# A weight slot given back in parts behind a pair of interleaved tiles

## The chip, the cores and the metric

The kernel runs on one core of one Trainium2 chip. The metric is the device time of one execution in microseconds (us), smaller is better. Five engines run side by side, each through its own list of instructions: TensorE (PE, matrix products), VectorE (DVE), ScalarE (ACT), GpSimd (POOL) and SyncE (SP, which here only starts transfers). They meet at counting semaphores alone. Matrix products land in PSUM, which has 8 banks of 512 floats per partition; two neighbouring banks are a "pair" here, and there are four pairs, 0 to 3.

## What is computed

Two transformer blocks over 1024 tokens of width 1024, in float32. Cut to what matters:

```python
# first block
xn   = rmsnorm(x) ; proj = xn @ w_in            # queries, keys, values, gated-delta inputs
h    = x + concat(windowed_attention, gated_delta_rule) @ w_out
h    = h + square(relu(rmsnorm(h) @ w_ffn_in)) @ w_ffn_out
# second block, on rmsnorm(h)
proj = rmsnorm(h) @ w_in_2                      # forgetting attention q k v f z, differential q k v z, gates
y    = gate_a * (ya @ w_branch[0]) + gate_b * (yb @ w_branch[1])
out  = h + rmsnorm(y @ w_out_2)
```

## The kernel before, in words

Every dense layer is cut into tiles of 128 output columns, numbered n = 0 to 159 through the whole program (N_OUT1 = 23, N_FFN = 31, N_FOX = 95 are the first tiles of the mixer's output, of the feed-forward layer and of the second block). A tile's weights are eight 128x128 blocks, one for each k of the 1024 input columns. Three steps bring a tile to PE:

- SP loads them into the raw slot `Wraw[:, n % 2]` (512 KB), once the tile two before has been split.
- POOL splits them into a rounded part and a remainder: a cast `Wh <- Wraw`, then a subtraction `Wl <- Wraw, Wh`. It may start when PE has finished tile n - 2, which used the same slot (semaphore `mm_done`), and posts `w_ready` when done.
- PE makes the tile with 48 matmuls: for each k three products (`Wh` by the high and by the low part of the input, `Wl` by the high part), each over two halves of 512 tokens. This is `product`. It waits for `w_ready` and, through `ps_free`, for the PSUM pair n % 2 to have been emptied by DVE or ACT.

Ordinarily PE makes one tile while POOL splits the next. At the start of four layers the input comes k by k from DVE and ACT. There `product_two` makes two tiles at once: for each k six matmuls of tile n, then six of tile n + 1. So both slots stay taken until the last k. These four places are called here by the tile pair made together: A (tiles 0 and 1, phase 1), B (N_OUT1, phase 5), C (N_FFN, phase 7) and D (N_FOX, phase 9).

In phase 1 the first five tiles are keys and queries. Their weights are loaded by `load_q` in two pieces whose rows are 64 floats long, on semaphores `q_in`, and split by `split_q`. Their results go to scratch memory (`bk_scr`, `bq_scr`) and come back as `bk` (`load_keys`, two transfers of 1 MB) and `bq` (`load_queries`). SP starts all of these in a written order and stops at each wait in it, so what stands behind a wait starts later. After tile 5 PE begins the windowed attention (`scores`, first matmul on line 676), with tiles 6 to 22 filled in between its steps.

In phase 9 two short matmul groups with `ones` spread per-token factors over the partitions: one (line 350) into pair 3, which DVE reads while it makes the input; and one (line 1875, from `dg1`) into pair 2, which DVE reads later, when it scales `hT`. DVE waits for the second one (`ms_done` 6) ahead of its first `st_l`, the operation that empties a PSUM pair there (line 1941) after ACT's `st_h` (line 1892).

Of the kernel before, what the change touches and what calls it, by code (L numbers as in the profile page):

```python
# [19 lines left out]
ALU = mybir.AluOpType  # L20
# [82 lines left out]
def build(nc, a, out):  # L103
    ctx = ExitStack()
    with ctx:
# [11 lines left out]
        def sem(name):  # L117
            return ctx.enter_context(nc.semaphore(name))
# [57 lines left out]
        def pair(s):  # L176
            return PS[:, 2 * s:2 * s + 2, :].rearrange("p b n -> p (b n)")
# [93 lines left out]

        def product(pe, n, slot, xs, x_ready=None):

            pe.wait_ge(w_ready, n + 1)
            if not (isinstance(n, int) and n < 2):
                pe.wait_ge(ps_free, n - 1)
            for c, (k, hi, lo) in enumerate(xs):
                if x_ready:
                    x_ready(k)
                for w, x, m in ((Wh, hi, 0), (Wh, lo, 1), (Wl, hi, 2)):  # L280
                    for b in range(2):
                        mm = pe.matmul(PS[:, 2 * slot + b, :], w[:, slot, k], x[:, b * 512:(b + 1) * 512],  # L282
                                       start=(c == 0 and m == 0), stop=(c == len(xs) - 1 and m == 2))
            mm.then_inc(mm_done, 1)
# [87 lines left out]
        def split_dve(dve, s0, w, row, spread=None):  # L372
# [23 lines left out]
            low(KT - 1)  # L396

        def product_two(pe, n, xs, ready, halves=False):

# [3 lines left out]
            for c, (k, hi, lo) in enumerate(xs):  # L403
# [10 lines left out]
                for i in range(2):  # L414
                    slot = (n + i) % 2
                    for w, x, m in ((Wh, hi, 0), (Wh, lo, 1), (Wl, hi, 2)):
                        for b in range(2):
                            mm = pe.matmul(PS[:, 2 * slot + b, :], w[:, slot, k], x[:, b * 512:(b + 1) * 512],  # L418
                                           start=(c == 0 and m == 0), stop=(c == len(xs) - 1 and m == 2))
                    if c == len(xs) - 1:  # L420
                        mm.then_inc(mm_done, 1)

        const_in, vec_in, x_in = sem("const_in"), sem("vec_in"), [sem(f"x_in{i}") for i in range(4)]
        par_in, filled = sem("par_in"), mixer_sem("filled")
        xT_done, xT_act, xT_dve = sem("xT_done"), sem("xT_act"), sem("xT_dve")
        pv_psum = sem("pv_psum")
        spill, x_back = sem("spill"), sem("x_back")
# [41 lines left out]
        def pe_phase0(pe):  # L469
# [12 lines left out]
            pe.wait_ge(vec_in, N_VEC)  # L482
            pe.transpose(PS[:, 4, 0:V_ROWS], vecs[:], ident[0:V_ROWS, 0:V_ROWS]).then_inc(pv_psum, 1)
            pe.wait_ge(acc_done, 1)
# [18 lines left out]
        def dve_phase0(dve):  # L503
# [3 lines left out]
            for g in BY_DVE:  # L507
                half, k = g // KT, g % KT
                dve.wait_ge(xT_done, g + 1)
                dve.tensor_copy(hT[:, k, half * 512:half * 512 + 512], PS[:, g % 4]).then_inc(xT_dve, 1)  # L510
            dve.wait_ge(pv_psum, 1)
            dve.tensor_copy(pv[:], PS[:, 4, 0:V_ROWS])
# [54 lines left out]
        def sp_phase1(sp):  # L567
# [6 lines left out]
            sp.wait_ge(line_sb, 1)  # L574
            sp.dma_start(line_one, line[:]).then_inc(line_out, 16)
            sp.wait_ge(bs_out[0], 32)
            load_keys(sp)
            sp.wait_ge(w_ready, 3)
            load_q(sp, 4)
            load_group(sp, N_ATT + 5, 1, a["w_in"], 640, loop=False)  # L580
# [49 lines left out]
        def pool_phase1(pool):  # L630
            pool.memset(cpad[0][:, 0:2], 0.0)
            pool.memset(cpad[0][:, S + 2:S + 4], 0.0)
            for j in range(2, 5):
                split_q(pool, j)
# [1018 lines left out]
        def pool_phase7(pool):  # L1653
            split(pool, N_FFN + 2, N_FOX + 2)

# [198 lines left out]
        def pool_phase9(pool):  # L1854
            split(pool, N_FOX + 2, N_VA)
            split_values(pool, N_VA, (va_h, va_l))

        h_final, m2_done = late_sem("h_final"), late_sem("second_norm_sum")
        dg1 = sb("dg1", [P, S], F32, R + 72)

        def pe_phase9(pe):
# [7 lines left out]
            for b in range(2):  # L1869
                pe.wait_ge(acc_done, 4 + b)  # L1870
                spread_half(pe, pair(3), facc[0], b).then_inc(ms_done, 1)
            product_two(pe, N_FOX, model, lambda k: pe.wait_ge(x_ready, 18 + k + 2), True)
            pe.wait_ge(acc_done, 6)
            for b in range(2):
                mm = pe.matmul(PS[:, 4 + b], ones[:], dg1[:, b * 512:(b + 1) * 512], start=True, stop=True)
            mm.then_inc(ms_done, 1)
            pairs(pe, N_FOX + 2, 6, lambda n, j, slot: product(pe, n, slot, model))
            product(pe, N_FGT, N_FGT % 2, model)
            value_products(pe, N_VA, (va_h, va_l))

        def act_phase9(act):
# [38 lines left out]
        def dve_phase9(dve):  # L1920
# [815 lines left out]
```

## Time and profile before

| what | value |
|---|---|
| median of 3 runs | 2551.58 us (2550.88 to 2552.43) |
| the profiled execution | 2553.9 us, of which the span of the trace is 2552.1 us |
| PE busy | 2441.5 us, 96% of the span |
| POOL busy | 689.7 us, 27% |
| DVE, ACT busy | 1002.2 us (39%), 723.1 us (28%) |
| mean granted TensorE clock | 0.972 of full |

A busy share of 96% leaves about 110 us in which PE does nothing. Each such stretch shows in the timeline of PE as an idle time in square brackets, with the instruction that ended it. Times in the timeline are microseconds from the span's start; the second number of a row is how long its group of instructions lasted. Steady pairs of 512-column matmuls start every 0.453 us, so one takes 0.227 us at full clock, and a tile of 48 takes 10.88 us.

### The profile page before, as it was taken

How to read it: one execution, taken by the hardware profiler on the slowest of the kernel's cores; microseconds unless marked ns; L12 is line 12 of the kernel's file. 1: busy time of each engine (PE TensorE's matmuls, PEld its weight loads, DVE VectorE, ACT ScalarE, POOL GpSimd, SP SyncE). 2: the span in 40 equal slices, each digit the busy share in tenths (PEclk: the TensorE clock that was granted, in tenths of full speed). 3: DMA queues.
4: the chain of work that ended last, by engine and by line, in shares of the span. 5: the costliest groups of instructions: out<-in, count | busy, mean ns of one | idle time of the engine just before them, and what ended most of it. 6: DMA issues, size and time to landing. Idle time of an engine off the chain costs nothing.

```text
span 2552.1 us, 33188 instructions
## 1 busy us (share of the span) xinstructions
PE 2441.5 (96%) x13182; PEld 2077.6 (81%) x13182; DVE 1002.2 (39%) x1479; ACT 723.1 (28%) x1147; POOL 689.7 (27%) x423
## 2 busy tenths in 40 slices
PE   6999996899898999999999999999999999999997
PEld 5788886899876888888888877988888788887886
DVE  4176634455535312212213344123333343557533
ACT  4144554122412100101101121135443113655022
POOL 2221112343322433333334322321111231111321
PEclk8999997899898999999999989999999999999998
DMA  6722212322330111111111115523441346524422
GB/s 206 205 58 67 67 51 68 92 57 57 133 107 25 58 50 42 49 49 49 49 49 49 47 35 187 169 62 91 120 118 51 130 165 145 134 65 149 149 91 91
DMA packets 257967, 232.11 MB, mean 91 GB/s; under 512 B 43233, under 2 KB 228359, under 8 KB 256312
## 3 DMA queue, kind: packets, MB, share of 16 engines
q1 hardware_dynamic: 234680, 170.65, 23.7%
q10 hardware_dynamic: 23168, 59.81, 6.5%
q8 instruction: 82, 1.34, 0.2%
q14 instruction: 37, 0.30, 0.0%
HBM read 167.41 MB, written 65.11 MB: 91 GB/s over the span
## 4 chain that ended last, share of the span: by engine, by line
PE 92%; DVE 2%; ACT 1%; DMA 1%; issue 1%; POOL 1%; POOLq 0%; ACTq 0%; DVEq 0%; SPq 0%; PEldq 0%; PEld 0%
PE PS L282 40%; PE PS L301 18%; PE PS L1828 4%; PE PS L2478 3%; PE PS L418 3%; PE PS L1783 3%; PE PS L2034 2%; PE PS L1320 2%; PE PS L1326 2%; PE PS L698 1%; PE PS L2023 1%; PE PS L2317 1%; PE PS L676 1%; PE PS L1337 1%; PE PS L686 1%
## 5 line engine op out<-in xcount | busy, mean ns | idle before, releaser
L253 POOL CAST Wh<-Wraw 128x1024 fp32r<-128x1024 f32 x144 | 150.8, 1047 | 1469.0 <-PE PS L282 619.3
L255 POOL TENSOR_TENSOR Wl<-Wraw,Wh 128x1024 fp32r<-128x1024 f32 x144 | 375.6, 2608 | 20.7
L1702 ACT ACTIVATE rbuf<-PS 128x1024 f32<-128x1024 f32 x32 | 32.9, 1028 | 493.7 <-PE PS L282 483.2
L282 PE MATMUL PS<-Fl,Wh 128*128 128x512 f32 x512 | 157.6, 389 | 0.0
L282 PE MATMUL PS<-Fh,Wh 128*128 128x512 f32 x512 | 157.6, 389 | 0.0
L282 PE MATMUL PS<-Fh,Wl 128*128 128x512 f32 x512 | 157.6, 389 | 0.0
L282 PE MATMUL PS<-XAh,Wh 128*128 128x512 f32 x440 | 139.7, 399 | 13.0 <-POOL Wl L255 6.0
L301 PE MATMUL PS<-XAh,Wh 128*128 128x512 f32 x328 | 134.8, 411 | 2.1 <-POOL Wl L255 2.1
L282 PE MATMUL PS<-XAl,Wh 128*128 128x512 f32 x440 | 136.1, 391 | 0.0
L282 PE MATMUL PS<-XAh,Wl 128*128 128x512 f32 x440 | 135.9, 390 | 0.0
L282 PE MATMUL PS<-XBh,Wh 128*128 128x512 f32 x440 | 135.5, 389 | 0.0
L282 PE MATMUL PS<-XBl,Wh 128*128 128x512 f32 x440 | 135.4, 389 | 0.0
L282 PE MATMUL PS<-XBh,Wl 128*128 128x512 f32 x440 | 135.4, 389 | 0.0
L301 PE MATMUL PS<-XAl,Wh 128*128 128x512 f32 x328 | 135.0, 412 | 0.0
L301 PE MATMUL PS<-XAh,Wl 128*128 128x512 f32 x328 | 134.6, 410 | 0.0
L301 PE MATMUL PS<-XBl,Wh 128*128 128x512 f32 x328 | 134.2, 409 | 0.0
L301 PE MATMUL PS<-XBh,Wh 128*128 128x512 f32 x328 | 133.6, 407 | 0.0
L301 PE MATMUL PS<-XBh,Wl 128*128 128x512 f32 x328 | 133.4, 407 | 0.0
L1732 DVE TENSOR_TENSOR rbuf<-rbuf 128x1024 f32<-128x1024 f32 x32 | 41.4, 1293 | 210.1 <-ACT rbuf L1702 210.1
L1742 DVE TENSOR_TENSOR hT<-hT,PS 128x1024 f32<-128x1024 f32 x24 | 29.3, 1221 | 218.3 <-PE PS L282 218.3
L282 PEld LDWEIGHTS PS<-Fl,Wh 128*128 128x128 f32 x512 | 96.1, 188 | 19.9
L282 PEld LDWEIGHTS PS<-Fh,Wl 128*128 128x128 f32 x512 | 96.1, 188 | 19.9
(431 smaller groups left out, 5416.4 us busy)
## 6 DMA issues: line engine op xcount, KB each, us to landing
Wraw<-in_w_in SPq DMA_DIRECT2D x66, 512.0 KB, 4.4
Wraw<-in_w_ffn_in SPq DMA_DIRECT2D x32, 512.0 KB, 4.0
Wraw<-in_w_ffn_out SPq DMA_DIRECT2D x32, 512.0 KB, 4.0
x_scr<-hT SPq DMA_DIRECT2D x2, 4096.0 KB, 14.2
Wraw<-in_w_out SPq DMA_DIRECT2D x16, 512.0 KB, 4.1
gate_scr<-gbuf ACTq DMA_DIRECT2D x16, 512.0 KB, 2.6
gin<-gate_scr ACTq DMA_DIRECT2D x8, 1024.0 KB, 7.3
xtok<-in_x SPq DMA_DIRECT2D x4, 1024.0 KB, 8.3
```

What stands on the lines that cost most here:

```text
L253: pool.tensor_copy(Wh[:, slot], Wraw[:, slot])
L255: pool.tensor_tensor(Wl[:, slot], Wraw[:, slot], Wh[:, slot].bitcast(F32), ALU.subtract).then_inc(w_ready, 1)
L282: mm = pe.matmul(PS[:, 2 * slot + b, :], w[:, slot, k], x[:, b * 512:(b + 1) * 512], start=(c == 0 and m == 0), stop=(c == len(xs) - 1 and ...
L301: mm = pe.matmul(PS[:, b, :], w[:, slot, k], x[:, b * 512:(b + 1) * 512], start=(c == 0 and m == 0), stop=(c == KT - 1 and m == 2))
L418: mm = pe.matmul(PS[:, 2 * slot + b, :], w[:, slot, k], x[:, b * 512:(b + 1) * 512], start=(c == 0 and m == 0), stop=(c == len(xs) - 1 and ...
L1320: mm = pe.matmul(bank(d, e)[:, h * 64:(h + 1) * 64], KdTs[p % 2][e][d][:, h], joined(W_of(p, e, d)[:, h], n, d), start=True, stop=True)
L1326: mm = pe.matmul(bank(d, e)[:, h * 64:(h + 1) * 64], U_of(p, e, d)[:, h], Xs[e][d][:, h, 0:64], start=True, stop=True)
L1732: dve.tensor_tensor(rbuf[:], rbuf[:], rbuf[:], ALU.mult).then_inc(f_sq, 1)
L1783: mm = pe.matmul(dst(c)[:, 0:w * P], q[:, i * P:(i + 1) * P], x[:, c * 512:c * 512 + w * P], start=(x is kh), stop=(x is kl and c != i // 4))
L1828: mm = pe.matmul(dst, x[:, at], w[:, :, k], start=(c == 0 and m == 0), stop=(c == KT - 1 and m == 2))
L2034: mm = pe.matmul(PS[:, 7, i * HD:(i + 1) * HD], aPT[:, p % 2, b * P:(b + 1) * P], vtok[:, k, h * HD:(h + 1) * HD], start=(k == 0), stop=(k ...
L2478: mm = pe.matmul(PS[:, 4 * (j % 2) + 2 * (k // 4) + b, :], w[:, slot, k], x[:, b * 512:(b + 1) * 512], start=(k % 4 == 0 and m == 0), stop ...
```

## The change

`product_two` posts a new semaphore, `first_parts`, when tile n has used its first six k blocks (`EARLY = 6`). POOL splits the next tile for that slot (n + 2) in two parts, by the new `split_behind_two`: blocks 0 to 5 on `first_parts`, blocks 6 and 7 on `mm_done` as before. This is done at all four places. In phase 1 SP now starts the load of tile 4 ahead of the keys. In phase 9 the spreading matmuls of `dg1` go ahead of `product_two`, and tile N_FOX + 2 is written to pair 3 instead of its usual pair, with ACT and DVE reading it there (`fox_bank`). One semaphore is saved by counting a transpose on `xT_done`.

```diff
-        def product(pe, n, slot, xs, x_ready=None):
+        def product(pe, n, slot, xs, x_ready=None, taken=None):
             pe.wait_ge(w_ready, n + 1)
-            if not (isinstance(n, int) and n < 2):
+            bank = slot
+            if taken is not None:
+                slot = n % 2
+                pe.wait_ge(ps_free, taken)
+            elif not (isinstance(n, int) and n < 2):
                 pe.wait_ge(ps_free, n - 1)
...
-                        mm = pe.matmul(PS[:, 2 * slot + b, :], w[:, slot, k], x[:, b * 512:(b + 1) * 512],
+                        mm = pe.matmul(PS[:, 2 * bank + b, :], w[:, slot, k], x[:, b * 512:(b + 1) * 512],
...
+        EARLY = 6
...
                     if c == len(xs) - 1:
                         mm.then_inc(mm_done, 1)
+                    elif c == EARLY - 1 and i == 0:
+                        mm.then_inc(first_parts, 1)
+
+        def split_behind_two(pool, n, x):
+            s = n % 2
+            for part, free, count in ((slice(0, EARLY), first_parts, x + 1), (slice(EARLY, KT), mm_done, n - 1)):
+                pool.wait_ge(free, count)
+                pool.tensor_copy(Wh[:, s, part], Wraw[:, s, part])
+                pool.drain()
+                ins = pool.tensor_tensor(Wl[:, s, part], Wraw[:, s, part], Wh[:, s, part].bitcast(F32), ALU.subtract)
+            ins.then_inc(w_ready, 1)
...
             sp.dma_start(line_one, line[:]).then_inc(line_out, 16)
+            sp.wait_ge(w_ready, 3)
+            load_q(sp, 4)
             sp.wait_ge(bs_out[0], 32)
             load_keys(sp)
-            sp.wait_ge(w_ready, 3)
-            load_q(sp, 4)
...
-            for j in range(2, 5):
+            pool.wait_ge(q_in[0], 64)
+            split_behind_two(pool, 2, 0)
+            for j in range(3, 5):
                 split_q(pool, j)
...
-            split(pool, N_OUT1 + 2, N_FFN + 2)
+            pool.wait_ge(w_in[N_OUT1 % 2], landed(N_OUT1 + 2))
+            split_behind_two(pool, N_OUT1 + 2, 1)
+            split(pool, N_OUT1 + 3, N_FFN + 2)
...
+        def fox_bank(j):
+            return pair(3 if j == 2 else (N_FOX + j) % 2)
...
-            product_two(pe, N_FOX, model, lambda k: pe.wait_ge(x_ready, 18 + k + 2), True)
             pe.wait_ge(acc_done, 6)
             for b in range(2):
                 mm = pe.matmul(PS[:, 4 + b], ones[:], dg1[:, b * 512:(b + 1) * 512], start=True, stop=True)
             mm.then_inc(ms_done, 1)
-            pairs(pe, N_FOX + 2, 6, lambda n, j, slot: product(pe, n, slot, model))
+            product_two(pe, N_FOX, model, lambda k: pe.wait_ge(x_ready, 18 + k + 2), True)
+            product(pe, N_FOX + 2, 3, model, taken=N_FOX)
+            product(pe, N_FOX + 3, (N_FOX + 3) % 2, model)
+            pairs(pe, N_FOX + 4, 4, lambda n, j, slot: product(pe, n, slot, model))
```

Places C and D have the same edit of POOL's list as B. What it makes of that list, for POOL at place A (tiles 2, 3 and 4), before and then now:

```order
L621 CAST Wh<-Wraw 128x1024 [waits mm_done,q_in0]
L623 TENSOR_TENSOR Wl<-Wraw,Wh 128x1024
L621 CAST Wh<-Wraw 128x1024 [waits mm_done,q_in1]
L623 TENSOR_TENSOR Wl<-Wraw,Wh 128x1024
L621 CAST Wh<-Wraw 128x1024 [waits mm_done,q_in0]
```

```order
L436 CAST Wh<-Wraw 128x768 [waits first_parts,q_in0]
L438 TENSOR_TENSOR Wl<-Wraw,Wh 128x768
L436 CAST Wh<-Wraw 128x256 [waits mm_done]
L438 TENSOR_TENSOR Wl<-Wraw,Wh 128x256
L639 CAST Wh<-Wraw 128x1024 [waits mm_done,q_in1]
L641 TENSOR_TENSOR Wl<-Wraw,Wh 128x1024
L639 CAST Wh<-Wraw 128x1024 [waits mm_done,q_in0]
```

Only tile 2 is split in two parts; tiles 3 and 4 wait as they did. SP's list in phase 1, where lines 443 and 461 are the loads of `load_q` and lines 606 and 624 those of the keys, before and then now:

```order
L575 DMA line_one<-line 8x512
L606 DMA bk<-bk_scr 64x4x1024 x2
L443 DMA Wraw<-in_w_in 128x8x64 x2
L208 DMA Wraw<-in_w_in 128x8x128
L582 DMA line_scr<-line_one 128x4096
```

```order
L593 DMA line_one<-line 8x512
L461 DMA Wraw<-in_w_in 128x8x64 x2
L624 DMA bk<-bk_scr 64x4x1024 x2
L208 DMA Wraw<-in_w_in 128x8x128
L600 DMA line_scr<-line_one 128x4096
```

Tile 4's two pieces have passed the two key transfers and nothing else. PE's list in phase 9, with the spread of `dg1` on line 1875 before and 1903 now; in between stand the remaining matmuls of `product_two` (line 418, now 424). First before:

```order
L350 MATMUL PS<-facc_138,ones 128x512 x2
L410 MATMUL PS<-XAh,Wh 128x512
...
L418 MATMUL PS<-XBh,Wl 128x512 x2
L1875 MATMUL PS<-dg_157,ones 128x512 x2
L195 UNCONDITIONAL_BRANCH
L195 ISA
L276 REGISTER_ALU
L282 MATMUL PS<-XAh,Wh 128x512 x2
```

Now:

```order
L354 MATMUL PS<-facc_138,ones 128x512 x2
L1903 MATMUL PS<-dg_157,ones 128x512 x2
L416 MATMUL PS<-XAh,Wh 128x512
...
L424 MATMUL PS<-XBh,Wl 128x512 x2
L286 MATMUL PS<-XAh,Wh 128x512 x2
```

The spread has moved from behind the pair of tiles to ahead of it, and the loop that held six tiles starts two tiles later.

## Rows read from the trace of the kernel before

**Rows 1.** Timelines of POOL, DVE, PE at A: start, us, engine, line, operation, [idle before].

```profile
53.95 1.04 POOL L621 CAST Wh<-Wraw 128x1024 fp32r<-128x1024 f32 x1 [26.51 <-PE PS L418]
54.96 1.23 DVE L825 SCALAR_TENSOR_TENSOR bst_l<-PS,bst_h 128x1024 fp32r<-128x1024 f32 x1 [7.48 <-ACT bst_h L738]
55.09 1.02 PE L652 MATMUL PS<-onehot,relb 33*8 33x512 f32 x2
57.53 0.73 PE L282 MATMUL PS<-XAh,Wh 128*128 128x512 f32 x2 [1.41 <-POOL Wl L623]
```

**Rows 2.** One line's instructions on POOL: duration in ns, least, median, most.

```profile
L645 POOL TENSOR_TENSOR Wl<-Wraw,Wh x1: 461/461/461, 351.0 to 351.0; 128x128 fp32r<-128x128 f32 x1
```

**Rows 3.** Timeline of PE: tile 3's end, tile 4, tile 5, the first scores.

```profile
78.97 0.61 PE L282 MATMUL PS<-XBh,Wl 128*128 128x512 f32 x2
83.78 1.22 PE L282 MATMUL PS<-XAh,Wh 128*128 128x512 f32 x2 [4.19 <-POOL Wl L623]
...
96.31 0.61 PE L282 MATMUL PS<-XAh,Wh 128*128 128x512 f32 x2
...
109.31 0.72 PE L676 MATMUL PS<-bk,bq 128*128 128x256 f32 x4
```

**Rows 4.** Timeline of SP's queue in phase 1: start and time to issue.

```profile
61.33 1.70 SPq L606 DMA_DIRECT2D bk<-bk_scr  x2
63.08 4.60 SPq L443 DMA_DIRECT2D Wraw<-in_w_in  x2
...
88.00 0.37 SPq L588 DMA_DIRECT2D bias<-line_scr  x1
104.18 2.58 SPq L614 DMA_DIRECT2D bq<-bq_scr  x4
```

**Rows 5.** DMA issues, windows 63:67.6, 40:43, 82.3:83, 99.2:100: KB, median us to landing.

```profile
Wraw<-in_w_in SPq DMA_DIRECT2D x2, 256.0 KB, 14.8
...
Wraw<-in_w_in SPq DMA_DIRECT2D x2, 256.0 KB, 6.1
...
bq_scr<-bst_l ACTq DMA_DIRECT2D x1, 512.0 KB, 8.1
...
bq_scr<-bst_l ACTq DMA_DIRECT2D x1, 512.0 KB, 4.9
```

**Rows 6.** Timelines of PE and DVE at B.

```profile
720.16 0.61 PE L418 MATMUL PS<-XBh,Wl 128*128 128x512 f32 x2
721.59 2.35 DVE L1639 TENSOR_TENSOR hT<-hT,PS 128x1024 f32<-128x1024 f32 x2 [12.20 <-DMA hT<-x_scr]
723.26 0.72 PE L282 MATMUL PS<-XAh,Wh 128*128 128x512 f32 x2 [2.49 <-POOL Wl L255]
```

**Rows 7.** Timelines of POOL, ACT and PE at C.

```profile
824.76 1.04 POOL L253 CAST Wh<-Wraw 128x1024 fp32r<-128x1024 f32 x1 [32.21 <-PE PS L418]
825.95 3.36 POOL L255 TENSOR_TENSOR Wl<-Wraw,Wh 128x1024 fp32r<-128x1024 f32 x1
...
824.81 1.03 ACT L1702 ACTIVATE rbuf<-PS 128x1024 f32<-128x1024 f32 x1 [8.28 <-PE PS L418]
...
829.44 0.73 PE L282 MATMUL PS<-XAh,Wh 128*128 128x512 f32 x2 [3.49 <-POOL Wl L255]
```

**Rows 8.** Timelines of PE and DVE at D.

```profile
1517.84 3.78 PE L350 MATMUL PS<-facc,ones 128*128 128x512 f32 x4 [2.65 <-DVE facc L361]
1524.35 0.76 PE L410 MATMUL PS<-XAh,Wh 128*128 128x512 f32 x1 [2.73 <-DVE XAl L378]
...
1547.69 1.88 PE L1875 MATMUL PS<-dg,ones 128*128 128x512 f32 x4
1550.94 0.73 PE L282 MATMUL PS<-XAh,Wh 128*128 128x512 f32 x2 [1.38 <-DVEq L1944]
...
1518.30 1.22 DVE L1935 TENSOR_TENSOR dg<-ident,sp 128x1024 f32<-128x1024 f32 x1
```

**Rows 9.** Windows at D: busy us of each engine, granted clock (PEclk), DMA share, GB/s.

```profile
1518.00:1524.00 6.00, 3.62 (x4) 1.01 (x4) 4.61 (x6) 1.63 (x3) 0.00 (x0) 0.50 0.00 0
1527.00:1528.00 1.00, 1.00 (x5) 0.78 (x4) 0.91 (x2) 0.26 (x1) 0.00 (x0) 0.79 0.00 0
```

More of the change, by code:

```diff
@@ L425, in build @@
         xT_done, xT_act, xT_dve = sem("xT_done"), sem("xT_act"), sem("xT_dve")
-        pv_psum = sem("pv_psum")
+        first_parts = sem("first_parts")
         spill, x_back = sem("spill"), sem("x_back")
@@ L482, in pe_phase0 @@
             pe.wait_ge(vec_in, N_VEC)
-            pe.transpose(PS[:, 4, 0:V_ROWS], vecs[:], ident[0:V_ROWS, 0:V_ROWS]).then_inc(pv_psum, 1)
+            pe.transpose(PS[:, 4, 0:V_ROWS], vecs[:], ident[0:V_ROWS, 0:V_ROWS]).then_inc(xT_done, 1)
             pe.wait_ge(acc_done, 1)
@@ L510, in dve_phase0 @@
                 dve.tensor_copy(hT[:, k, half * 512:half * 512 + 512], PS[:, g % 4]).then_inc(xT_dve, 1)
-            dve.wait_ge(pv_psum, 1)
+            dve.wait_ge(xT_done, 2 * KT + 1)
             dve.tensor_copy(pv[:], PS[:, 4, 0:V_ROWS])
@@ L1653, in pool_phase7 @@
         def pool_phase7(pool):
-            split(pool, N_FFN + 2, N_FOX + 2)
+            pool.wait_ge(w_in[N_FFN % 2], landed(N_FFN + 2))
+            split_behind_two(pool, N_FFN + 2, 2)
+            split(pool, N_FFN + 3, N_FOX + 2)
         def pe_phase7(pe):
@@ L1854, in pool_phase9 @@
         def pool_phase9(pool):
-            split(pool, N_FOX + 2, N_VA)
+            pool.wait_ge(w_in[N_FOX % 2], landed(N_FOX + 2))
+            split_behind_two(pool, N_FOX + 2, 3)
+            split(pool, N_FOX + 3, N_VA)
             split_values(pool, N_VA, (va_h, va_l))
+        def fox_bank(j):
+            return pair(3 if j == 2 else (N_FOX + j) % 2)
         h_final, m2_done = late_sem("h_final"), late_sem("second_norm_sum")
@@ L1891, in act_phase9 @@
                     act.wait_ge(qk_out[j % 2], 32 * (j // 2))
-                act.activation(st_h[:, j % 2], pair(n % 2), ACT.Copy, scale=-0.125 if j < 4 else 1.0).then_inc(qk_hi, 1)
+                act.activation(st_h[:, j % 2], fox_bank(j), ACT.Copy, scale=-0.125 if j < 4 else 1.0).then_inc(qk_hi, 1)
                 act.wait_ge(qk_hi, j + 1)
@@ L1940, in dve_phase9 @@
                 dve.wait_ge(qk_hi, j + 1)
-                dve.scalar_tensor_tensor(st_l[:, j % 2], pair((N_FOX + j) % 2), -0.125 if j < 4 else 1.0,
+                dve.scalar_tensor_tensor(st_l[:, j % 2], fox_bank(j), -0.125 if j < 4 else 1.0,
                                          st_h[:, j % 2].bitcast(F32), ALU.mult, ALU.subtract).then_inc(qk_lo, 1)
```

## The prediction

> **What bounds the kernel now.** I read the busy shares first: PE is busy for 96% of the span, so only the holes in PE's timeline, and stretches in which its clock is low, can be won back. Then I read PE's timeline around the four pairs of tiles. Each has a hole behind it, shown by the idle time in brackets: 1.41 us at A, 2.49 at B, 3.49 at C, 1.38 at D [rows 1, 6, 7, 8]. A fifth and largest hole, 4.19 us, stands ahead of tile 4 in phase 1 [rows 3]. Of each I then asked which wait ends next if the one named is removed, in the timelines of POOL, DVE and ACT, and for the fifth in SP's queue and the landings.
>
> **The slot given back in parts: POOL's side.** At A the split starts at 53.95, on the end of tile 0, about 1.1 us before PE's stream for the pair ends (the next matmul starts at 55.09). PE starts tile 2 at 57.53, so whole split and wake-up take 3.58 us [rows 1]: cast 1.04, a pause of 0.15 (824.76 + 1.04 to 825.95, [rows 7]), subtraction and wake-up 2.39. Now only two blocks of eight are left at that moment. Their cast is a quarter, 0.26; the pause stays; the subtraction lies between a quarter, 0.6, and what the 128-column one says: 0.46 for one block [rows 2] and about 0.27 for each further, so 0.73. With 0.1 for the wake-up that is 1.1 to 1.25; for a fixed cost in the cast I take 1.3. So the slot is ready 0.2 us after the pair ends. The first part, three quarters of 3.58 or 2.7 us, begins when 30 of the pair's 96 matmuls are left, 6.8 us at 0.227, and must be done in the 5.7 us before tile n's end: it is hidden, with 3 us to spare. It adds one cast, one subtraction and one pause to POOL, which idled for 26 us there [rows 1]. PE's matmuls are the same ones.
>
> **A, tile 2.** The slot is ready at 53.95 + 1.3 = 55.25. But tile 2 needs PSUM pair 0, which DVE has read at 54.96 + 1.23 = 56.19, and line 652 ends at 55.09 + 1.02 = 56.11 [rows 1]. So PE starts at 56.3: gain 57.53 - 56.3 = 1.2.
>
> **A, tile 4.** Its two pieces are issued at 63.08, behind 2 MB of keys, and take 14.8 us to land [rows 4, 5]; PE waits until 83.78, while tile 3's stream ends at 78.97 + 0.45 = 79.42 [rows 3]. Moved up, they are issued at 61.33, where the keys stood. PE now wants tile 4 at 79.42 - 1.2 = 78.2, so they must land by 78.2 - 3.6 = 74.6, 13.3 us after issue. The nearest row, pieces of this size behind another transfer that had just ended, took 6.1 [rows 5]; the same 14.8 as before would leave a hole of about 3 us. I take that the hole is gone: 4.36. It also cost clock: tile 4 took 96.31 - 83.78 = 12.53 instead of 10.88 [rows 3], because PE restarted at half clock; 1.65 comes back. A is now ahead by 1.2 + 4.36 + 1.65 = 7.2 at tile 5.
>
> What is late next there? The first scores (109.31, wanted at 102.1 now) need the keys, the bias and the first queries. The keys are started some 4 us later than 61.33 but wanted 36 us later: hidden. The queries are issued at 104.18, when the stores of tile 4's result have landed; the second store took 4.9 us from its issue at about 99.3 on an idle DMA, while the one before it, among other traffic, took 8.1 [rows 4, 5]. The stores now start 7.2 us sooner, at 92.1, beside the bias load that is issued at 88.00 and is not sooner. Between 4.9 and 8.1 I take 6.2, since the bias is then half landed: queries issued at 98.3 instead of 97.0. That is 1.3 late, of which some 0.4 was slack (their issue and landing end at about 108.9). PE waits 0.9. A gives 7.2 - 0.9 = 6.3; ends 4.0 (8.1 us store) and 7.2.
>
> **B.** Ready at 720.16 + 0.45 + 0.2 = 720.8 instead of 723.26. But tile N_OUT1 + 2 also needs PSUM pair 1 of tile N_OUT1, and DVE empties it only from 721.59, having waited 12.20 us for the 4 MB of `hT` to come back; its two operations take 2.35, the first ends at 722.8 [rows 6]. That DMA starts on DVE's work, which the change does not touch. PE starts at 722.9: gain 0.3, not 2.4.
>
> **C.** The split starts at 824.76; ready at 826.06 instead of 829.44. ACT empties the PSUM pair at 824.81 + 1.03 = 825.84 [rows 7], earlier. Gain 3.4. The subtraction took 3.36 us here and not 2.4: DVE squared `rbuf` at the same time. Now POOL's short subtraction starts at about 825.2, before ACT's copy has ended and so before DVE's square; if DVE came first, it would cost POOL one DVE operation, 1.2 us, and C would give 2.2. The SBUF — State Buffer page of the Trainium skill ("Who interferes with whom") says that DVE with two SBUF inputs and GpSimd lock one port pair against each other for a whole instruction, whoever starts first. By that rule C is 3.4 or 2.2, nothing between, and the longer subtraction in the trace agrees with it. The slot-1 split that now follows at once may hold DVE's square up; DVE has a whole tile, 10.9 us, for a chain of about 6.
>
> **D.** Before, three things stood between the pair's end (1547.69) and tile N_FOX + 2 (1550.94): the spread of `dg1`, 1.88 us; POOL; and DVE's emptying of the pair, which ended last [rows 8]. All three go: the spread moves ahead, the tile gets pair 3, POOL is ready 1.3 after a release at 1547.69 - 1.1 = 1546.6, so at 1547.9. That is 3.0 us. The price is the spread ahead of the pair. DVE has `dg1` ready at 1518.30 + 1.22 = 1519.5. PE's first spread ends at 1517.84 + 3.78 = 1521.62, and PE idles 2.73 us until 1524.35 [rows 8]. At half clock the moved one takes 3.78, as its twin does, and ends at 1525.4, 1.05 late; at full clock it takes 1.88 and fits. The granted clock is 0.50 (1.2 GHz) up to 1524 and rises to full (2.4 GHz) within 1527:1528 [rows 9], some 3 us after PE restarts at 1524.35. Behind the hole of tile 4 it rose after 1.65 / 0.5 = 3.3 us of half speed. Now PE runs without a hole from 1517.84, so by these two I expect full clock by about 1523, the moved spread done by 1524.35, and the first block of the pair (12 matmuls, before 7 slow and 5 fast, 4.1 us) at full clock, 2.7 us. Of that 1.4 I take 1.0, since DVE needs two operations of 1.2 us for the next block. Below, no earlier rise: 1.05 late, of which the 2.4 matmuls moved from half to full clock return half, so 0.55 lost; at worst 1.05. D gives 3.0 + 1.0 = 4.0; ends 2.0 and 4.4. TensorE: Matmul & The Clock Gate ("What's actually happening") in the Trainium skill says that activity releases the throttle. By that rule filling the hole makes the clock rise sooner and D is worth 4.0, without it 2.5; the half clock in [rows 9] while PE had holes agrees.
>
> **Sum.** 6.3 + 0.3 + 3.4 + 4.0 = 14.0 us. The loops that start a tile later, the dropped `slot_open` posts and the shared semaphore change instructions on engines that idle there: nothing. The profiled execution took 2553.9 us (2552.1 of span, 1.8 around it), which gives 2539.9. It was 2.3 above the median of 2551.58, so the median should be **2537.6 us**. Between the four places PE shows no hole in which an earlier start could be lost again before the next fixed event; a gain at one place is carried to the end.
>
> **Rivals.**
> 1. The clock at D does not rise sooner. For it: at D full clock came only at 1527, ten us after 1517.84. Against: a hole lay between. D gives 2.5, sum 12.5: 2539.1.
> 2. Phase 1 gives part back: the tile-4 pieces land late, or the stores beside the bias take 8.1 us and the first scores wait for queries. For it: the DMA rows of that stretch, 14.8 and 8.1 [rows 5]. A gives about 3.5, sum 11.2: 2540.4.
> 3. The change doesn't do what it says: the first part is not done when tile n ends, so the slot is ready as late as before. For it nothing in the rows; POOL has 5.7 us for 2.7. Then A gives 4.36 + 1.65 - 0.9 = 5.1, B and C nothing, D 1.7 (0.7, POOL's full split ending 3.6 after the release, and the 1.0 of the clock), sum 6.8: 2544.8.
> 4. Slower: the keys, now behind 2048 short rows and with the line table and bias behind them, land so late that `scores` waits. The order of bytes is the same for all but the keys, so it would take a queue that slows down as a whole. It decides from a landing past 102.1 and turns the sum negative only past 102.1 + 14 = 116, 35 us later than the slowest piece of before landed. At 120 it would be 2555.5.
>
> **How the numbers follow.** Forecast 0.62, rival 1 0.18, rival 2 0.14, rival 3 0.04, rival 4 0.02. The likeliest case alone spans 2536 to 2539. For the range: all best ends give 7.2 + 0.3 + 3.4 + 4.4 = 15.3, 2536.3, less a run's spread of 0.8, so 2535.3; the worst ends of A, C and D give 4.0 + 0.3 + 2.2 + 2.0 = 8.5, 2543.1. This leaves out rivals 3 and 4. About 0.2%, 5.1 us, is what a measurement of this kernel can tell from no change: faster by more than that 0.95, within it 0.03, slower 0.02.
>
> **What would show it.** In the trace after: tile 2 starting about 1.2 us behind the pair's end at A, held by DVE; no idle ahead of tile 4 and full clock through it; `bq` issued near 98; at B a hole of about 2.2 us that still ends with DVE and `hT`; at C and D holes under 0.5 us; full clock before 1525 less the shift at D. Wrong would be: a wait on `Wraw` ahead of tile 4, a wait of scores on keys or bias, a second part longer than 1.5 us, or a hole behind tile N_FOX + 2 or + 3 for PSUM.

## The result and the profile after

| | before | after |
|---|---|---|
| median of 5 runs each on one chip, us | 2552.43 (2550.88 to 2554.57) | 2539.39 (2537.82 to 2540.67) |
| ratio after / before, 95% interval | | 0.9948 (0.9937 to 0.9958) |
| profiled execution / its span, us | 2553.9 / 2552.1 | 2537.8 / 2536.0 |
| mean granted clock in the profile | 0.972 | 0.976 |

The kernel became 13.0 us faster by the medians and 16.1 by the two profiled executions; 14.0 was forecast, as 2537.6 us. The median came out 1.8 us above that, of which 0.85 is that the kernel before has a median of 2552.43 here and had one of 2551.58 there. Line numbers of the new kernel are 4 to 28 higher: L436 and L438 are the new split in parts, L286 and L424 the old L282 and L418, L672 the old L652.

**A.** Timelines of POOL, DVE and PE (start, us, engine, line, operation, [idle before <- who ended it]), the answer to [rows 1]:

```profile
47.28 0.83 POOL L436 CAST Wh<-Wraw 128x768 fp32r<-128x768 f32 x1 [20.03 <-PE PS L424]
48.25 1.85 POOL L438 TENSOR_TENSOR Wl<-Wraw,Wh 128x768 fp32r<-128x768 f32 x1
52.65 0.40 POOL L436 CAST Wh<-Wraw 128x256 fp32r<-128x256 f32 x1 [2.55 <-PE PS L424]
53.19 0.74 POOL L438 TENSOR_TENSOR Wl<-Wraw,Wh 128x256 fp32r<-128x256 f32 x1
```

```profile
53.73 1.23 DVE L845 SCALAR_TENSOR_TENSOR bst_l<-PS,bst_h 128x1024 fp32r<-128x1024 f32 x1 [6.45 <-ACT bst_h L758]
```

```profile
53.87 1.02 PE L672 MATMUL PS<-onehot,relb 33*8 33x512 f32 x2
55.16 0.70 PE L286 MATMUL PS<-XAh,Wh 128*128 128x512 f32 x2 [0.27 <-DVEq L848]
77.04 0.61 PE L286 MATMUL PS<-XAh,Wh 128*128 128x512 f32 x2
87.92 0.61 PE L286 MATMUL PS<-XAh,Wh 128*128 128x512 f32 x2
```

The first part is done at 50.10, the second at 53.93, six hundredths after L672 starts. PE is then held by DVE, until 54.96. Tile 4 starts at 77.04 with no idle time in its row and lasts 10.88 us, all of it at full clock; before it lasted 12.53 [rows 3].

SP's queue and the landings, the answer to [rows 4, 5], and what PE waits for then:

```profile
60.10 1.77 SPq L461 DMA_DIRECT2D Wraw<-in_w_in  x2
61.92 1.63 SPq L624 DMA_DIRECT2D bk<-bk_scr  x2
86.55 0.38 SPq L606 DMA_DIRECT2D bias<-line_scr  x1
97.35 2.59 SPq L632 DMA_DIRECT2D bq<-bq_scr  x4
```

```profile
Wraw<-in_w_in SPq DMA_DIRECT2D x2, 256.0 KB, 4.4
...
bq_scr<-bst_l ACTq DMA_DIRECT2D x1, 512.0 KB, 6.5
```

```profile
103.03 0.71 PE L696 MATMUL PS<-bk,bq 128*128 128x256 f32 x4 [1.86 <-DMA bq<-bq_scr]
...
104.97 0.38 PE L706 MATMUL PS<-ident,wS 128*128 128x128 f32 x2
```

```profile
101.88 1.28 ACT L799 ACT_TABLE_LOAD   x1
```

The pieces of tile 4 land 4.4 us after their issue (before 14.8) and the scores now wait 1.86 us for the queries. ACT's load of a table (the last fence) falls into that wait. L706 is the first turn of the scores: there PE transposes the first weights `wS`, which ACT has made behind that table.

**B.** Timelines of DVE and PE, the answer to [rows 6]:

```profile
712.99 0.61 PE L424 MATMUL PS<-XBh,Wl 128*128 128x512 f32 x2
...
715.81 0.95 PE L286 MATMUL PS<-XAh,Wh 128*128 128x512 f32 x2 [2.20 <-DVE hT L1661]
716.56 1.05 PE L286 MATMUL PS<-XAl,Wh 128*128 128x512 f32 x2
```

```profile
714.53 2.35 DVE L1661 TENSOR_TENSOR hT<-hT,PS 128x1024 f32<-128x1024 f32 x2 [12.33 <-DMA hT<-x_scr]
```

The hole is left, and DVE, which waits for `hT`, ends it. Two matmuls now take 1.05 us and not 0.62: PE restarts at half clock, which it did not in the profile before. The pair itself also took longer. Its start in PE's timeline, before and then now:

```profile
695.87 1.20 PE L418 MATMUL PS<-XAh,Wh 128*128 128x512 f32 x2
```

```profile
687.43 1.20 PE L424 MATMUL PS<-XAh,Wh 128*128 128x512 f32 x2
```

With its last matmul at 720.16 and at 712.99 that makes 24.74 us before and 26.01 now, with the rise to full clock later in it.

**C.** Timelines of POOL, PE and DVE, the answer to [rows 7]:

```profile
817.28 0.40 POOL L436 CAST Wh<-Wraw 128x256 fp32r<-128x256 f32 x1 [2.55 <-PE PS L424]
817.83 0.74 POOL L438 TENSOR_TENSOR Wl<-Wraw,Wh 128x256 fp32r<-128x256 f32 x1
```

```profile
818.70 0.72 PE L286 MATMUL PS<-XAh,Wh 128*128 128x512 f32 x2
```

```profile
820.85 3.39 DVE L1758 TENSOR_TENSOR Fl<-rbuf,Fh 128x1024 fp32r<-128x1024 f32 x1 [1.13 <-ACT Fh L1728]
```

POOL's short subtraction takes 0.74 us, as at A, and PE starts with no idle time in the row. The collision has moved: DVE's `Fl`, an operation that takes about 1.2 us alone, now takes 3.39 beside POOL's next split.

**D.** Timeline of PE, the answer to [rows 8], and the windows of [rows 9] (busy us of PE, PEld, DVE, ACT, POOL, then the granted clock):

```profile
1505.90 3.78 PE L354 MATMUL PS<-facc,ones 128*128 128x512 f32 x4 [2.65 <-DVE facc L365]
1509.48 2.87 PE L1903 MATMUL PS<-dg,ones 128*128 128x512 f32 x4
1512.41 0.47 PE L416 MATMUL PS<-XAh,Wh 128*128 128x512 f32 x1
...
1534.15 0.61 PE L424 MATMUL PS<-XBh,Wl 128*128 128x512 f32 x2
1534.81 0.73 PE L286 MATMUL PS<-XAh,Wh 128*128 128x512 f32 x2
```

```profile
1505.90:1508.50 2.60, 2.60 (x3) 1.18 (x4) 2.17 (x3) 0.00 (x0) 0.00 (x0) 0.50 0.00 0
1511.00:1513.00 2.00, 1.94 (x6) 0.86 (x5) 1.91 (x4) 1.19 (x2) 0.00 (x0) 0.89 0.00 0
```

The moved spread takes 2.87 us, between 3.78 (half clock, 1.2 GHz) and 1.88 (full, 2.4 GHz): the clock rises within it. The pair starts 6.51 us after the first spread, as it did before, but at full clock.

The same stretches in both profiles, in us, from the starts in PE's timeline:

| stretch | before | after | gain |
|---|---|---|---|
| A: pair's end (L672 starts) to tile 2 | 2.44 | 1.29 | 1.15 |
| tile 2 to tile 5 | 38.78 | 32.76 | 6.02 |
| tile 5 to the first turn of scores | 15.90 | 17.05 | -1.15 |
| B: the hole | 2.65 | 2.37 | 0.28 |
| B: the next six tiles | 65.43 | 66.99 | -1.56 |
| C: the hole | 3.66 | 0.29 | 3.37 |
| D: the pair | 23.33 | 22.19 | 1.14 |
| D: pair's end to next tile | 3.26 | 0.21 | 3.05 |
| pairs at A, B, C; column sums ahead of D | 87.52 | 85.09 | 2.43 |

In the last row the pairs at A and C and the column sums (short matmuls with `ones`) vary from profile to profile, as the runs below show; the pair at B (1.27 us longer now) is another matter, taken up under B further down.

### The profile page after: what moved, and what is told of

Its sections match the earlier page's. It is cut to its first block, busy times and chain, and to the rows that moved or that the text cites. A ratio compares the mean times of both kernels' runs of the same rounds, so it can differ in the third digit from the quotient of the medians.

```text
span 2536.0 us, 33223 instructions
## 1 busy us (share of the span) xinstructions
PE 2437.3 (96%) x13182; PEld 2073.2 (82%) x13182; DVE 997.9 (39%) x1479; ACT 723.1 (29%) x1147; POOL 691.3 (27%) x431
## 4 chain that ended last, share of the span: by engine, by line
PE 91%; DVE 3%; DMA 2%; ACT 1%; issue 1%; POOL 0%; POOLq 0%; DVEq 0%; SPq 0%; ACTq 0%; PEldq 0%; PEld 0%
PE PS L286 40%; PE PS L305 18%; PE PS L1852 4%; PE PS L2509 3%; PE PS L1807 3%; PE PS L2065 2%; PE PS L424 2%; PE PS L1346 2%; PE PS L1340 2%; PE PS L718 1%; PE PS L2054 1%; PE PS L2348 1%; PE PS L696 1%; PE PS L1357 1%; PE PS L706 1%
## 5 line engine op out<-in xcount | busy, mean ns | idle before, releaser
L255 POOL TENSOR_TENSOR Wl<-Wraw,Wh 128x1024 fp32r<-128x1024 f32 x141 | 367.5, 2607 | 20.3
L286 PE MATMUL PS<-Fh,Wl 128*128 128x512 f32 x512 | 157.6, 389 | 0.0
L286 PE MATMUL PS<-Fl,Wh 128*128 128x512 f32 x512 | 157.6, 389 | 0.0
L286 PE MATMUL PS<-Fh,Wh 128*128 128x512 f32 x512 | 157.6, 389 | 0.0
L286 PE MATMUL PS<-XAh,Wh 128*128 128x512 f32 x440 | 139.7, 399 | 2.6 <-DVE hT L1661 2.2
L286 PE MATMUL PS<-XAl,Wh 128*128 128x512 f32 x440 | 136.3, 391 | 0.0
L286 PE MATMUL PS<-XAh,Wl 128*128 128x512 f32 x440 | 135.9, 390 | 0.0
L286 PE MATMUL PS<-XBh,Wl 128*128 128x512 f32 x440 | 135.5, 389 | 0.0
L286 PE MATMUL PS<-XBh,Wh 128*128 128x512 f32 x440 | 135.5, 389 | 0.0
L286 PE MATMUL PS<-XBl,Wh 128*128 128x512 f32 x440 | 135.4, 389 | 0.0
L286 PEld LDWEIGHTS PS<-Fh,Wl 128*128 128x128 f32 x512 | 96.1, 188 | 20.0
L286 PEld LDWEIGHTS PS<-Fh,Wh 128*128 128x128 f32 x512 | 96.1, 188 | 20.0
## 6 DMA issues: line engine op xcount, KB each, us to landing
x_scr<-hT SPq DMA_DIRECT2D x2, 4096.0 KB, 14.8
```

Of the source, the lines that this page charges most:

```text
L255: pool.tensor_tensor(Wl[:, slot], Wraw[:, slot], Wh[:, slot].bitcast(F32), ALU.subtract).then_inc(w_ready, 1)
L286: mm = pe.matmul(PS[:, 2 * bank + b, :], w[:, slot, k], x[:, b * 512:(b + 1) * 512], start=(c == 0 and m == 0), stop=(c == len(xs) - 1 and ...
```

## The experiments

The first four kernels ran together on one chip, and the last four on another. Every diff is against the changed kernel. The kernel before took 2555.78 us in the first group and 2554.65 in the second, each some 2 to 3 above its median beside the changed kernel, so whole times are compared by their ratio to before (for the changed kernel 0.9948, a gain of 13.3 us); the last column is the difference from that, x 2552.

| kernel | runs | median, us | ratio to before (95%) | against the changed kernel by ratio, us |
|---|---|---|---|---|
| e1 | 5 | 2546.46 | 0.9969 (0.9955 to 0.9983) | 5.4 slower |
| e2 | 4 | 2541.74 | 0.9945 (0.9928 to 0.9962) | 0.8 faster |
| e3 | 7 | 2547.24 | 0.9968 (0.9957 to 0.9979) | 5.1 slower |
| e4 | 4 | 2537.02 | 0.9931 (0.9914 to 0.9948) | 4.3 faster |
| e5 | 1 | 2544.54 | | |
| e6 | 1 | 2542.19 | | |
| e7 | 5 | 2534.14 | 0.9923 (0.991 to 0.9937) | 6.4 faster |
| e8 | 5 | 2539.04 | 0.9946 (0.9931 to 0.996) | 0.5 faster |

An interval is 5 to 9 us wide, and a figure of the last column carries the error of two ratios, some 4 to 5 us either way. So e1, e3 and e7 differ from the changed kernel by whole times, e2 and e4 don't, and small terms are read from the profiles. Positions in phase 1 are compared as distances from the pair's end (the start of L672), since what lies ahead of it varies from profile to profile.

**e1: the keys ahead of tile 4's pieces again.**

```
-            sp.wait_ge(w_ready, 3)
-            load_q(sp, 4)
             sp.wait_ge(bs_out[0], 32)
             load_keys(sp)
+            sp.wait_ge(w_ready, 3)
+            load_q(sp, 4)
```

> The changed kernel with SP's order of before in phase 1: keys first, then tile 4's weights. My theory: the hole ahead of tile 4 comes back with its half-clock restart (4.4 + 1.65 us, and the 1.15 us won at tile 2 is lost in it), while the wait of the first scores for queries goes; tile 5 starts about 32.8 + 6 = 39 us behind tile 2 or later, and the whole is 6 us slower than the changed kernel. Rival: the hole was due to the pieces' own short rows and not to the 2 MB ahead of them: then tile 4 still has no hole, nothing lost.

Measured: 5.4 us slower than the changed kernel by the ratios (7.1 by the medians). PE's timeline, and the landing of the pieces:

```profile
83.50 1.22 PE L286 MATMUL PS<-XAh,Wh 128*128 128x512 f32 x2 [5.65 <-POOL Wl L641]
84.52 1.06 PE L286 MATMUL PS<-XAl,Wh 128*128 128x512 f32 x2
```

```profile
Wraw<-in_w_in SPq DMA_DIRECT2D x2, 256.0 KB, 15.9
```

The hole and the half clock behind it are back, and what tile 2 had won is waited out there: the hole is 5.65 and not 4.19. The order of the two loads alone is worth most of A's gain; without it the earlier tile 2 is worth nothing. The scores follow tile 2 by 54.44 us against 47.87, and the first turn comes 58.63 us behind the pair's end, against 51.10 in the changed kernel and 57.12 before.

**e2: D as before (spread behind the pair, the old PSUM pair), the split still in parts.**

```
-            return pair(3 if j == 2 else (N_FOX + j) % 2)
+            return pair((N_FOX + j) % 2)
```
```
+            product_two(pe, N_FOX, model, lambda k: pe.wait_ge(x_ready, 18 + k + 2), True)
             ...    the spread of dg1
-            product_two(pe, N_FOX, model, lambda k: pe.wait_ge(x_ready, 18 + k + 2), True)
-            product(pe, N_FOX + 2, 3, model, taken=N_FOX)
-            product(pe, N_FOX + 3, (N_FOX + 3) % 2, model)
-            pairs(pe, N_FOX + 4, 4, lambda n, j, slot: product(pe, n, slot, model))
+            pairs(pe, N_FOX + 2, 6, lambda n, j, slot: product(pe, n, slot, model))
```

> The changed kernel with D as before but for the split in parts: the dg1 spread behind the pair, tile N_FOX + 2 in its usual PSUM pair. Theory: the split alone is worth nothing at D, because DVE empties the pair only after the spread; the hole behind the spread is 1.4 us as before, the first block of the pair runs partly at half clock again, and D loses all of its 4.2 us. Rival: the clock is a matter of chance and not of the hole that the spread fills: then the first block is at full clock here too and D loses 3.0.

Measured: by whole times it can't be told from the changed kernel (2.4 us slower by the medians, 0.8 faster by the ratios), so D's 4.2 are not confirmed there; the gain over the kernel before, 14.0 us (9.7 to 18.4), even leaves out by a little the 9.1 that 13.3 - 4.2 makes. The profile tells more. Timelines of PE, POOL and DVE:

```profile
1512.80 0.76 PE L416 MATMUL PS<-XAh,Wh 128*128 128x512 f32 x1 [2.73 <-DVE XAl L382]
...
1537.42 1.88 PE L1904 MATMUL PS<-dg,ones 128*128 128x512 f32 x4
```

```profile
1536.83 0.74 POOL L438 TENSOR_TENSOR Wl<-Wraw,Wh 128x256 fp32r<-128x256 f32 x1
```

```profile
1539.34 1.23 DVE L1970 SCALAR_TENSOR_TENSOR st_l<-PS,st_h 128x1024 fp32r<-128x1024 f32 x1 [9.81 <-PE PS L1904]
```

The 2.73 us hole ahead of the pair is back and the pair starts at half clock (24.62 us long; in the profile before, behind the same hole, 23.33; with the spread in that hole 22.2 in all eight profiles). POOL has the slot ready at 1537.57, yet the next tile starts at 1540.68, 3.26 us after the pair's end, exactly as before: DVE is idle 9.81 us for the spread and then has 1.23 to do. So at D the split in parts gains nothing until both other waits are gone. From first spread to next tile it is 34.39 us here, 33.10 before, 28.91 with the change.

**e3: all four splits whole again, everything else as changed.**

```
-            split_behind_two(pool, N_FFN + 2, 2)
-            split(pool, N_FFN + 3, N_FOX + 2)
+            split(pool, N_FFN + 2, N_FOX + 2)
...
```

> The changed kernel with the slot split whole at all four places, as before. Theory, by place: A 1.15, B 0.3, C 3.4, D 2.4 us lost (POOL's split then ends 3.6 us after the release), sum 7.2 us slower than the changed kernel. Rival: POOL's split no longer sets anything at A and D since PSUM and the pair 3 do: then only C is lost, 3.4.

Measured: 5.1 us slower by the ratios (7.9 by the medians). PE's timeline at A, C and D:

```profile
57.45 0.74 PE L286 MATMUL PS<-XAh,Wh 128*128 128x512 f32 x2 [1.41 <-POOL Wl L641]
...
826.03 0.72 PE L286 MATMUL PS<-XAh,Wh 128*128 128x512 f32 x2 [3.48 <-POOL Wl L255]
...
1545.89 0.73 PE L286 MATMUL PS<-XAh,Wh 128*128 128x512 f32 x2 [2.40 <-POOL Wl L255]
```

The holes grow by 1.14 at A, 0.29 at B, 3.36 at C and 2.35 at D. The first doesn't reach the end against the first profile of the changed kernel: the first turn comes 51.10 us behind the pair's end in both. Here PE does not wait for the queries; there the stores and the queries' load take the head start. In e8, the changed kernel again, the wait is short, the turn comes after 49.97, and A's 1.1 is kept. Without A's tile 2 the stretches come to 0.3 + 3.4 + 2.4 = 6.0 us, with it to 7.1; the whole times can't tell the two apart. The first spread at D to the next tile takes 31.30 us, 1.80 less than before; the third rival had 1.7 for this case.

**e4: `hT` comes back in two DMAs, so that B's first operation of DVE needs only the first.**

```
-            sp.dma_start(hT[:], x_scr).then_inc(x_back, 16)
+            sp.dma_start(hT[:, 0:2], x_scr[:, 0:2]).then_inc(x_back, 16)
+            sp.dma_start(hT[:, 2:KT], x_scr[:, 2:KT]).then_inc(const_in, 16)
```
```
+                if j == 2:
+                    dve.wait_ge(const_in, 32)
```

> The changed kernel with the return of hT in phase 5 as two transfers, its first two of eight rows of tiles (1 MB) first, and DVE waiting for these alone ahead of the first two tiles. Theory: B's hole is DVE's wait for 4 MB; the first MB lands some 9 us sooner, the hole falls from 2.2 to about 0.3 us and PE's clock does not fall behind it: 2 to 3.5 us faster than the changed kernel. Rival: the hole is set by something else as late (POOL, or the second transfer, which tile 2 of the phase then waits for): less than 0.5 us.

Measured: 4.3 us faster by the ratios (2.4 by the medians), within the error. PE's timeline at B:

```profile
715.99 0.61 PE L424 MATMUL PS<-XBh,Wl 128*128 128x512 f32 x2
716.74 0.72 PE L286 MATMUL PS<-XAh,Wh 128*128 128x512 f32 x2
```

The hole falls from 2.37 to 0.30, as expected, and the next six tiles take 65.41 us instead of 66.99, since the clock doesn't fall: 2.07 + 1.58 = 3.65 us in this profile, and the same in e7.

**e5: the bias load behind the queries.**

```
-            sp.dma_start(bias[:], ...).then_inc(bias_in, 16)
             sp.wait_ge(bs_out[0], 96)
             load_queries(sp, 0)
+            sp.dma_start(bias[:], ...).then_inc(bias_in, 16)
```

> The changed kernel with the 1.5 MB bias load issued behind the first queries instead of ahead of tile 4's stores. Theory: these stores took 6.5 us because the bias load ran beside them; alone they take about 4.9, the queries are issued 1.6 us sooner and PE's wait of 1.86 us for them is gone; DVE then waits for the bias instead, until about 106. Rival: the stores are slow from what SP queued earlier (line table, tile 6): then they still take over 6 us and the wait for queries stays.

One run, 5.5 us above e8. Timelines of SP, DVE and PE:

```profile
96.03 2.58 SPq L632 DMA_DIRECT2D bq<-bq_scr  x4
98.66 0.61 SPq L609 DMA_DIRECT2D bias<-line_scr  x1
```

```profile
106.06 0.48 DVE L873 CUSTOM_DVE_ANT_0 wS<-PS,bias,rows 128x256 f32<-128x256 f32 x1 [15.44 <-DMA bias<-line_scr]
```

```profile
100.94 0.71 PE L696 MATMUL PS<-bk,bq 128*128 128x256 f32 x4
...
107.24 0.69 PE L706 MATMUL PS<-ident,wS 128*128 128x128 f32 x2 [4.23 <-ACT wS L799]
```

Without the bias beside them the stores let the queries go 5.3 us after the last store's issue at 90.73, where the changed kernel needs 6.5 (90.85 to 97.35), and PE's wait of 1.86 is gone. The bias comes too late instead: the first turn is at 107.24 and not 104.97, partly at half clock, and by the third turn 4.4 us are lost (116.54 against 112.10). That the bias load slows the stores is seen in the other profiles too. Where the last store is issued 4.2 to 4.3 us behind the bias load (the changed kernel, e2, e4), the queries go 6.3 to 6.5 us after it; at 4.7 and 4.8 (e6, e8) it is 6.0 and 5.7; at 5.9 (e3) and 11.2 (before) it is 4.9. So the bias load is in the way of the stores, but it can't simply go last.

**e6: the first part four blocks instead of six.**

```
-        EARLY = 6
+        EARLY = 4
```

> The changed kernel with EARLY = 4: half of the slot is left for after the release. Theory, from the second part's 0.40 + 0.14 + 0.74 us for two blocks: 0.7 us more for four, so the hole at C grows from 0.29 to 1.0 and at D from 0.21 to 0.9, while A (held by PSUM at 0.27) and B (held by hT at 2.4) stay: 1.4 us in all. Rival: the holes at C and D are PE's own restart and PSUM, not POOL: they stay under 0.4.

One run, 3.2 us above e8, of which the two holes below are 1.5. POOL's second part at C:

```profile
818.88 0.61 POOL L436 CAST Wh<-Wraw 128x512 fp32r<-128x512 f32 x1 [8.59 <-PE PS L424]
819.64 1.28 POOL L438 TENSOR_TENSOR Wl<-Wraw,Wh 128x512 fp32r<-128x512 f32 x1
```

The holes are 1.04 at C and 0.96 at D, 0.75 more each, and nothing more at A and B (1.29, 2.52), where DVE ends the wait. The cut matters only where POOL ends last.

**e7: e4, and the bias in two halves, the second behind the queries.**

```
-            sp.dma_start(bias[:], ...).then_inc(bias_in, 16)
+            sp.dma_start(bias[:, 0:4], ...).then_inc(bias_in, 16)
             sp.wait_ge(bs_out[0], 96)
             load_queries(sp, 0)
+            sp.dma_start(bias[:, 4:8], ...).then_inc(par_in, 16)
```
```
+                if u == 4:
+                    dve.wait_ge(par_in, N_PAR + 16)
```

> The changed kernel with hT in two transfers as tried before, and the bias of heads 4 to 7 loaded behind the first queries. Theory: half the bias (0.75 MB) has landed before tile 4's stores start; the scores start at about 101.2 instead of 103, but ScalarE's table load, which the wait hid, is on the path again: net 0.9 us; with hT's 3.7 us in all 4.6 faster than the changed kernel, 18 than before. Rival: the second half of the bias, now behind the queries, holds DVE up at head 4: then nothing from the bias.

Measured: 2534.14 us (2531.79 to 2535.87), 4.9 below e8 on the same chip. The hole at B is 0.30 and the six tiles 65.39. Timelines of SP and PE in phase 1:

```profile
96.03 2.60 SPq L634 DMA_DIRECT2D bq<-bq_scr  x4
```

```profile
100.94 0.71 PE L698 MATMUL PS<-bk,bq 128*128 128x256 f32 x4
...
103.58 0.44 PE L708 MATMUL PS<-ident,wS 128*128 128x128 f32 x2 [0.52 <-ACT wS L801]
```

PE doesn't wait for the queries. Yet the first turn is no earlier than in e8. The pair's end and the first turn, in e7 and then in e8:

```profile
53.62 1.02 PE L674 MATMUL PS<-onehot,relb 33*8 33x512 f32 x2
```

```profile
54.79 1.02 PE L672 MATMUL PS<-onehot,relb 33*8 33x512 f32 x2
...
104.76 0.44 PE L706 MATMUL PS<-ident,wS 128*128 128x128 f32 x2
```

The turn comes 49.96 us behind the pair's end in e7 and 49.97 in e8, where PE still waits 0.43 us for the queries; in the first profile of the changed kernel it is 51.10. ACT sets the turn in both: its table load starts 48.0 us behind the pair's end (at 101.62 and 102.81), takes 1.28, and its first `wS` comes behind it. The short wait for the queries is hidden beside that. So what halving the bias is worth is not shown: nothing against e8, 1.1 against the first profile. Of the 4.9 us below e8, B's hole and clock are 1.93 + 1.61 = 3.5 in the profiles. The kernel as a whole is faster than the changed one: its slowest run (2535.87) lies below the fastest of e8 (2538.46).

**e8: the changed kernel once more,** to see which stretches repeat.

> The changed kernel itself, on the same chip as the others. Theory: the stretches without an idle wait that differ between profiles differ by PE's clock alone and by chance: the pair at A takes 23.3 to 24.6 us, that at C 23.2 or 24.7, while the pair at D stays at 22.2 and the stretch of six tiles behind B's hole at 67.0 or 65.4. Rival: they are set by the code: then all repeat the first profile of the changed kernel (23.32, 23.23, 22.19, 66.99).

Measured: 2539.04 us (2538.46 to 2543.58), the changed kernel's time again; span of the profile 2537.6. The pair at A took 24.09 us (23.32 in the first profile), at C 24.68 (23.23), at D 22.23 (22.19), the six tiles behind B 67.00 (66.99), the pair at B 25.61 (26.01), and the queries' wait was 0.43 (1.86). Over all ten profiles the pairs at A and C vary by 1.3 and 1.5 us with the moment at which the clock rises, whatever the kernel; D and the six tiles repeat.

## Why the prediction was right

**The second part of the split.** 0.26 + 0.15 + 0.73 was forecast; 0.40 + 0.14 + 0.74 came. Small casts have a fixed cost, which the taken 1.3 us covered. The first part was hidden everywhere (2.55 us of POOL's idle time lie behind it at A, B and C, 1.67 at D).

**A, tile 2.** Forecast 1.2, held by DVE; measured 1.15, held by DVE. That PE is really held by POOL with a whole split is shown by e3. How much of the 1.15 is left at the first turn depends on the wait for the queries.

**A, tile 4.** Forecast 4.36 + 1.65 = 6.0; measured 6.02, and e1 shows that the order of the loads makes it. The landing took 4.4 us, less than the 6.1 taken from the nearest row; 13.3 would have done. The prediction's hole of "about 3 us" for a landing of 14.8 does not follow from its own numbers, which give 61.33 + 14.8 - 74.6 = 1.5; only the second rival hangs on it. The keys were issued 1.8 us after tile 4's pieces, where 4 had been said, and nothing waited for them.

**The queries.** Forecast a wait of 0.9. In the first profile it was 1.86, in the four others with the same loads and an early tile 2 (e2, e4, e6, e8) 0.94, 1.29, 0.66 and 0.43, a mean of 1.04 over the five. The reason, stores beside the bias load, holds: they took 6.5 us for the 6.2 taken, and the less of the bias load there was beside them, the less they took (e5's rows and those beside it). The prediction left out ACT's table load ahead of the first turn, though PE idled 0.81 us there before the change as well. It stands on the path as soon as PE doesn't wait, so a wait removed there is worth less than its length. In the first profile 2.11 us were lost at the start of the scores, and 0.96 of them came back at the first turn. For the whole of A, 6.3 was forecast: the first turn comes 57.12 us behind the pair's end before, and 51.10, 51.72, 50.54, 49.96 and 49.97 in the same five profiles, a mean gain of 6.5.

**B.** Forecast 0.3, with DVE and `hT` as the end; measured 0.28, and e4 shows the cause. The step that missed something is the statement that an earlier start can't be lost before the next fixed event: in the changed kernel the clock fell behind this hole, 1.56 us over six tiles. It did so in seven of the eight profiles with the hole; before's is the one in which it did not, and in none of the two without the hole. The pair at B shows the same: 24.74 us before, and 25.6 to 26.2 in all nine profiles of the other kernels, though its matmuls are the same. Together that is up to 2.8 us more at B than forecast. Whether the change causes it, by the moment at which PE arrives there, or whether the one profile of the kernel before met a good clock twice, is open, since it was profiled once.

**C.** Forecast 3.4; measured 3.37, and 3.36 given back in e3. POOL's short subtraction was over 0.07 us after DVE's square began (817.83 + 0.74, 818.50), so the two hardly met. The meeting came one step later: POOL's next subtraction starts at 820.77 and lasts 2.40 us, DVE's `Fl` starts at 820.85 and lasts 3.39 instead of 1.23, that is, until 1.07 us after POOL's end. The SBUF — State Buffer page ("Who interferes with whom") in the Trainium skill says that the order of issue decides who blocks. These rows agree, as the later one of the two was held. It is harmless here, as DVE had the room.

**D.** Forecast 3.0 + 1.0; measured 3.05 + 1.14. The pair is 22.2 us long in all eight profiles with the spread ahead and 23.33 and 24.62 in the two with the hole. That the clock rises sooner when the hole is filled, the reason that the first rival denied, is so shown in the repeats too. The rise fell within the moved spread, near 1511.5 by its 2.87 us, 5.5 after the first spread, where "about 1523" had said 5.2; by the lengths of the spreads it came 3.3 to 6.0 us after the first spread's start in all eight. With the hole it came 9.4 (before) and 11.9 us (e2) after it. TensorE: Matmul & The Clock Gate ("What's actually happening") in the Trainium skill says that activity releases the throttle. These numbers agree.

**The sum.** The forecast terms measure 1.15 + 6.02 - 1.15 + 0.28 + 3.37 + 4.19 = 13.9 us for 14.0. The profiles lie 16.1 apart because pairs and column sums elsewhere met a better clock in the second profile (2.43 in the last row of the table, less the 1.56 behind B, and 1.4 spread over the rest); for A, C and the column sums the ten profiles show that such lengths are chance. The medians lie 13.0 apart (13.3 by the ratio, and 13.8 in e8). The 1.0 between is within what five runs can tell. A median above the forecast would fit the clock lost at B, but no run isolates it in whole times. So the terms were right one by one, within some tenths; that nothing was lost between them was not, and how near the total came is in part luck. Two ends of the prediction are also off by its own numbers: A's lower end is 7.2 - (1.3 + 1.9 - 0.4) = 4.4, not 4.0, and the lower end of the range is 2536.3 - 0.8 = 2535.5, not 2535.3. Neither matters here.

**The rivals.** The first fails at D. The second is half right, the queries are waited for, but the pieces of tile 4 landed early. The third, a slot ready as late as before, was run as e3: by its ratio a gain of 8.2 us (5.4 to 11.0) where it had 6.8. The changed kernel has 13.3 (10.7 to 16.1), and the holes at C and D come back in e3 as said, so the split in parts does what it says. The fourth, late keys, is seen in no profile.

## What to carry to other kernels

Where two streams end together, give a shared slot back in parts so that only a short piece is behind the last use, but look in each place at who ends last: it was worth 3.4 us where POOL did, 0.3 where DVE waited for a transfer, nothing at D until two other waits had gone, and at A 1.1 that a later wait for the queries could take back. A small load that is wanted soon belongs ahead of a large one that is wanted late, and a load placed beside stores on which the next load hangs slows them; whether cutting it in parts pays was not shown. A hole can also cost clock in the stream behind it (tile 4, B, D), though it did not behind C's 3.7 us, so work that can be moved into a hole may be worth more than the hole. Two profiles are best compared stretch by stretch, each from an event just ahead of it: by their own clocks e7 seemed to win 1.2 us at the first turn that were won elsewhere by chance.

## What the runs showed of the hardware

- Two pieces of 256 KB landed in 4.4 us with no large load ahead of them on SP's queue, and in 14.8 and 15.9 us behind 2 MB on the same queue.
- From the issue of the last 512 KB store to that of the queries, which wait for it, 6.3 to 6.5 us passed where the 1.5 MB bias load had been issued 4.2 to 4.3 us ahead of it, 5.7 and 6.0 at 4.8 and 4.7, and 4.9 at 5.9 and 11.2.
- Behind B's hole of 2.2 to 2.7 us, between streams at full clock, PE restarted at half clock in seven of eight profiles; behind a hole of 0.3 in neither of two. Behind C's hole of 3.7 us (before, e3) it went on at full clock, so the hole's length alone does not tell.
- One kernel's pairs of tiles differ by up to 1.5 us from profile to profile, with the moment at which the clock rises. By that, an estimate: a difference of spans below some 3 us between two single profiles says nothing without the stretches.
- POOL's cast took 0.40, 0.61, 0.83 and 1.04 us for 256, 512, 768 and 1024 columns, its subtraction 0.74, 1.28, 1.85 and 2.35.
